# Expert weights in 2 MB slots, and an earlier load of one vector of rows, in a two-block transformer kernel

## The reference, cut to what matters

```
for l in range(DEPTH):                                   # DEPTH = 1
    mod = cond @ w_ada[l] + b_ada[l]                     # 6 x 1024 columns
    sh_m, sc_m, g_m, sh_f, sc_f, g_f = jnp.split(mod[:, None, :], 6, axis=-1)
    h = _rms(x, norm_mix[l]) * (1.0 + sc_m) + sh_m
    proj = h @ w_in[l]
    ...
    x = x + g_m * (mixed @ w_out[l])
    h = _rms(x, norm_ffn[l]) * (1.0 + sc_f) + sh_f
    x = x + g_f * _moe(h, w_router[l], b_router[l], w_gu[l], b_gu[l], w_dn[l], b_dn[l])
```

## Time and profile before

| what | value |
|---|---|
| median of 3 runs | 2108.74 us (2106.86 to 2115.24) |
| the profiled execution | 2115.58 us |
| its span | 2113.9 us |
| PE busy | 1990.8 us (94%) |
| DVE, ACT busy | 597.1 us, 409.4 us |
| DMA | 582.22 MB, 275 GB/s over the span |
| granted PE clock, mean | 0.972 |

### The profile page before, as it was taken

How to read it: one execution, slowest core, us unless ns; L and a number is a source line. 1 busy time by engine, 2 the same in 40 slices (tenths; PEclk the granted TensorE clock), 3 DMA queues, 4 the chain that set the end, 5 groups by cost and what they waited for, 6 DMA issues and landing times.

```text
span 2113.9 us, 23652 instructions
## 1 busy us (share of the span) xinstructions
PE 1990.8 (94%) x9060; PEld 1130.5 (53%) x9060; DVE 597.1 (28%) x1240; ACT 409.4 (19%) x868; POOL 93.0 (4%) x166
## 2 busy tenths in 40 slices
PE   6889999999899998899899988999999999999998
PEld 2665877433333333333233333756888456668863
DVE  1277522222211221112112211443333025433311
ACT  2124321211010111111011111243221023421110
POOL 0000000000000000000000000110000011000000
PEclk9989999999999999999999999999999999999999
DMA  9564557899999999999999998252544333344430
GB/s 376 154 224 166 170 191 288 349 420 420 421 421 420 421 420 421 421 421 420 421 421 421 421 421 352 100 199 87 178 145 158 139 130 134 122 143 159 148 141 31
DMA packets 160453, 582.22 MB, mean 275 GB/s; under 512 B 12936, under 2 KB 59144, under 8 KB 110080
## 3 DMA queue, kind: packets, MB, share of 16 engines
q1 hardware_dynamic: 155312, 574.71, 69.2%
q0 software_dynamic: 5072, 6.56, 1.4%
HBM read 578.60 MB, written 2.62 MB: 275 GB/s over the span
## 4 chain that ended last, share of the span: by engine, by line
PE 72%; DMA 21%; SPq 5%; ACT 1%; issue 1%; DVE 1%; POOL 0%; DVEq 0%; ACTq 0%
PE psum L358 52%; DMA work<-w_gu 9%; DMA ring<-w_gu 9%; PE psum L607 9%; PE psum L654 8%; SPq L466 5%; DMA gain_rows<-b_ada 2%; PE psum L2077 1%; PE psum L644 1%; DMA ring<-w_in 1%; PE psum L633 1%; DMA ring<-w_ada 0%; ACT work L2398 0%; PE psum L1027 0%; PE psum L560 0%
## 5 line engine op out<-in xcount | busy, mean ns | idle before, releaser
L358 PE MATMUL psum<-normed,ring 128*128 128x256 f32 (+1 forms) x2432 | 510.4, 372 | 0.2 <-PE psum L358 0.2
L358 PEld LDWEIGHTS psum<-normed,ring 128*128 128x128 f32 x2432 | 445.1, 192 | 61.7 <-issue 5.0
L607 PE MATMUL psum<-work,normed 128*64 128x512 f32 x1024 | 241.2, 629 | 38.6 <-DMA work<-w_gu 38.6
L607 PE MATMUL psum<-ring,normed 128*64 128x512 f32 x1024 | 237.5, 620 | 32.3 <-DMA ring<-w_gu 31.7
L358 PE MATMUL psum<-ring,work 128*128 128x512 f32 (+1 forms) x592 | 249.8, 581 | 0.1
L358 PE MATMUL psum<-work 128*128 128x128 f32 (+7 forms) x1152 | 186.1, 334 | 18.6 <-DVE gain_rows L1567 14.6
L607 PEld LDWEIGHTS psum<-work,normed 128*64 128x64 f32 x1024 | 77.0, 145 | 200.7 <-issue 200.7
L358 PEld LDWEIGHTS psum<-ring,work 128*128 128x128 f32 x592 | 111.7, 190 | 130.6 <-issue 129.3
L358 PEld LDWEIGHTS psum<-work 128*128 128x128 f32 (+2 forms) x1152 | 135.7, 187 | 80.7 <-issue 52.9
L607 PEld LDWEIGHTS psum<-ring,normed 128*64 128x64 f32 x1024 | 76.4, 143 | 190.7 <-issue 189.0
L358 PE MATMUL psum<-ring,normed 128*128 128x512 f32 (+2 forms) x400 | 160.5, 556 | 2.2 <-DMA ring<-w_in 1.7
(11 more groups left out here) (303 smaller groups left out, 1332.4 us busy)
## 6 DMA issues: line engine op xcount, KB each, us to landing
ring<-w_gu SPq DMA_DIRECT2D x128, 1024.0 KB, 26.3
work<-w_gu SPq DMA_DIRECT2D x128, 1024.0 KB, 26.3
ring<-w_dn SPq DMA_DIRECT2D x64, 1024.0 KB, 26.8
work<-w_dn SPq DMA_DIRECT2D x64, 1024.0 KB, 26.8
ring<-w_in SPq DMA_DIRECT2D x25, 2048.0 KB, 12.5
ring<-w_up SPq DMA_DIRECT2D x44, 1024.0 KB, 7.2
ring<-w_ada SPq DMA_DIRECT2D x11, 2048.0 KB, 9.2
ring<-w_down SPq DMA_DIRECT2D x10, 2048.0 KB, 7.7
```

Of the source, the lines that this page charges most:

```text
L358: return pe.matmul(out, lhsT, rhs, start=first, stop=last, **kw)
L607: ins = pe.matmul(b[r], self.hgT[:, o, r], ws[e][:, n0:n0 + 512], start=o == 0, stop=o == EIGHTHS - 1, skip_group_check=True)
```

## The change

1. **Slots of 2 MB.** The weights of a pair come in 12 pieces of 2 MB: quarter q of w_gu of expert e, and half of w_dn. A partition's part is one run of 16 KB. PE still makes the same products in the same order, but waits once for a quarter, and signals its use once (`quarter_used`, `down_half`); a slot is refilled when the slot 8 places before has been used.
2. **First refill and last w_dn half in two pieces.** The first refill (first half of w_dn of the first pair, into the slots of quarter 0) is issued as 2 x 2 pieces of 1 MB: the first two when eighth 0 has been used (`first_eighth`), the other two when the quarter has been. The last w_dn half of the last pair is also issued in pieces of 1 MB, and PE waits for the second pieces apart (`rest_in`).
3. **b_ada rows.** `bias_rows(2)` is the first DMA of POOL's queue and waits only for `("win", 0)`, the first slice of w_in.
4. **Bias line.** The line goes to DRAM once (8 x 384 numbers) and is spread there by a DMA from DRAM to DRAM, 128 rows of 3072 numbers; `toeplitz` reads from that.
5. **Turns.** The turn of the probabilities stands before `ada(6)` and `ada(7)`; `attend(1)` stands behind the first two turns of x; `y_transposes(1)` stands before the last `attn_out`. The bank list and ACT's list are put in the same order.

```diff
-EIGHTHS, DOWN_PARTS = 8, 4
+QUARTERS = 4
 def pair_slots(u):
-    return [("gu", u, o, e) for o in range(EIGHTHS) for e in range(2)] + [("wd", u, m, e) for m in range(DOWN_PARTS) for e in range(2)]
+    return [("gu", u, q, e) for q in range(QUARTERS) for e in range(2)] + [("wd", u, half, e) for half in range(2) for e in range(2)]
...
+        if kind == "gu":
+            src = io["w_gu"][bass.ds(2 * p + e, 1), part * 256:part * 256 + 256, :]
+            sp.dma_start(slot(S.no(name), 2, 2048), src.rearrange("a (p k) n -> p (a k) n", p=P)).then_inc(*S.fills(*name))
+            return
...
+    def load_by_halves(self, sp, io, S, slot, names, p, between=None):
+        for m in range(2):
+            for name in names:
+                part, e = name[2:]
+                src = io["w_dn"][bass.ds(2 * p + e, 1), part * 512:part * 512 + 512, :].rearrange("a (p m k) n -> m p (a k) n", p=P, m=2)
+                sp.dma_start(slot(S.no(name), 4, 1024)[:, 2 * m:2 * m + 2], src[m])\
+                    .then_inc(*(S.fills(*name) if m == 0 else (self.rest_in[part], 16)))
+            if m == 0 and between is not None:
+                sp.wait_ge(*between)
...
+            if i < MOE_SLOTS + 2 and skip:
+                if name[3] == 0:
+                    sp.wait_ge(self.first_eighth, 1)
+                    self.load_by_halves(sp, io, S, slot, PAIR_SLOTS[i:i + 2], pair, (self.quarter_used, 1))
+                continue
             if name[3] == 0:
-                earlier = i - PIECES
+                earlier = i - MOE_SLOTS
...
+        for q in range(QUARTERS):
+            pe.wait_ge(self.rows_ready, it * 4 * TWINS + (4 * u + q + 1))
+            ws = []
+            for e in range(2):
+                pe.wait_ge(*S.ready("gu", u, q, e, it=it))
+                ws.append(mem.slot(S.no(("gu", u, q, e)), 2, 2048))
+            if q < QUARTERS - 1:
+                for k in range(2):
+                    for c in range(4):
...
+        pool.wait_ge(*S.ready("win", 0))
+        bias_rows(2)
         pool.wait_ge(line_ready, 1)
-        pool.dma_start(line, line_sb.unsqueeze(1).to_broadcast([HEADS, P, 384])).then_inc(line_out, 16)
-        bias_rows(2)
+        pool.dma_start(line_one.rearrange("a (h n) -> (a h) n", h=HEADS), line_sb).then_inc(line_out, 16)
         pool.wait_ge(line_out, 16)
+        pool.dma_start(line, line_one.to_broadcast([P, HEADS * 384])).then_inc(line_out, 16)
+        pool.wait_ge(line_out, 32)
         pool.wait_ge(*B.ready("kT", 1))
...
         logits(0)
         by_token(("z", 0), wait_slot("win", 6), 0, 512)
+        turn_probs(0)
         ada(6)
         attend(0)
...
         by_token(("z", 1), wait_slot("win", 7), 0, 512)
+        turn_probs(1)
         ada(7)
-        attend(1)
         for t in range(NT):
+            if t == 1:
+                attend(1)
...
         attn_out((2,))
         ada(11)
+        y_transposes(1)
         attn_out((3,))
         mod_rows(11)
-        y_transposes(1)
```

More of the change, by code:

```diff
@@ L455, in __init__, with load @@
         assert A.at <= WORK - (MOE_SLOTS - SLOTS) * SLOT
-    def load(self, sp, io, S, name, p):
+    def load(self, sp, io, S, slot, name, p):
         kind, u, part, e = name
[L460 to L466, removed]
@@ L471, in last_use, with load_weights @@
+    def load_weights(self, sp, io, S, B, slot, pair, it, skip=0, last=False):
         def last_use(name, it, turn):
             kind, u, part, e = name
[L474 to L477, removed]
+            if kind == "gu" and part < QUARTERS - 1:
+                return self.quarter_used, (it - turn) * 3 * TWINS + (3 * u + part + 1)
+            if kind == "wd" and part == 0:
+                return self.down_half, (it - turn) * TWINS + (u + 1)
@@ L595, in weights_and_biases, with column @@
                           start=False, stop=False, skip_group_check=True)
[L597 to L602, removed]
+        def column(c, q, k, ws):
             b = psum[:, B.no(columns[c])]
@@ L645, in products @@
                       start=True, stop=False, skip_group_check=True)
[L646 to L651, removed]
+        for half in range(2):
+            pe.wait_ge(*B.released("aT", u, half, it=it))
+            ws = []
+            for e in range(2):
+                pe.wait_ge(*S.ready("wd", u, half, e, it=it))
+                ws.append(mem.slot(S.no(("wd", u, half, e)), 4, 1024))
+            for k, dh in [(k, dh) for k in range(4) for dh in range(2)][0:8 - 4 * half] + [(k, dh) for dh in range(2) for k in (2, 3)][0:4 * half]:
+                if (k, dh) == (2, 0):
+                    pe.wait_ge(self.rest_in[half], it * 32 * TWINS + 32 * (u + 1))
                 for e in range(2):
                     r = slice(e * CAP, (e + 1) * CAP)
[L654 to L656 removed]
+                    ins = pe.matmul(psum[r, B.no(("dn", u, dh))], self.actT[:, 4 * half + k, r], ws[e][:, k, dh * 512:dh * 512 + 512],
+                                    start=False, stop=half == 1 and k == 3, skip_group_check=True)
+                if half == 1 and k == 3:
                     ins.then_inc(*B.fills("dn", u, dh))
[L658 to L659 removed]
+            if half == 0:
+                ins.then_inc(self.down_half, 1)
     def act_part(self, act, B, psum, it, u):
@@ L1903, in second_block @@
     bank_free = [sem(f"bank_free_2_{b}") for b in range(BANKS)]
+    slot_full = [sem(f"slot_full_2_{b}") for b in range(SLOTS)]
     LL = range(LAYERS)
```

139 lines of the change are left out of this document (72 added, 67 removed).

## The result

The changed kernel takes **2078.47 us** (median of four executions, 2075.91 to 2079.24), the kernel before 2110.76 us on the same chip (four executions). The ratio is 0.9848, with a 95% interval of 0.9826 to 0.9870. 2077 us and a gain of 31.9 us were forecast; the gain is 32.3 us.

The account below looks back on a forecast made before the run. DMA engines were taken to bound the experts, PE mostly the rest. 18.3 + 3.6 + 12 - 2 = 31.9 us off the 2108.7 us median gave 2077 us, range 2066 to 2096 us.

Parts of the forecast that it names:

- The rows and the line: Front: loading the b_ada rows early removes PE's wait before the last `dots` group and its after-effects, 18.3 us; spread line 0 us.
- The 14.64 us: Front: PE's standstill before the fourth `dots` group, while DVE waits for the b_ada rows, goes whole.
- the 0.85 us: Front: the last `dots` group's four matmuls follow the twelve before in 0.3 us, not 1.15 us.
- The 2.8 us of slow clock: Front: the 64 matmuls after the wait take 13.98 us at full clock, not 16.79 us.
- late next: Front: next candidate is the w_in slice issued at 89.38 us, wanted at about 119 us, expected in at 109 us.
- The bounds of the margins: Front: w_in slice in at 109 us, spread line by 97 us, early load covered, DVE not the new wait.
- The turns: First block: three PE waits for ACT's copies, before `O` 0, `O` 1 and `ys`, go: 3.6 us, at least 0.
- The rate: Experts: 16 KB rows move 1.5% faster than 8 KB rows; 13.4 us worked out, 12 us taken, bounds 0 and 14.
- The dip: Experts' first refills: the next refill waits for the whole quarter and the DMA queue runs empty, 2 us lost, between 0 and 3.
- The rival of little gain in rate: Experts: 16 KB rows bring only 0 to 0.6%, total 2084 to 2089 us; chance 0.18.
- the slower one: Experts: long rows move worse, so the rate falls; chance 0.10, of which 0.06 slower overall.
- The front's wait: Front: the wait returns as late w_in, late `bias` or DVE's pace; half the 18.3 us left gives 2086 us; chance 0.10.

Follow-up runs that it names:

- a_slots_only: Kernel before with only the 2 MB slots and split loads, front as before: 2094.56 us, ratio 0.9932.
- a_turns_only: Kernel before with only the turns of the first block in their new order: 2106.97 us, ratio 0.9993.
- c_old_turns: Changed kernel with the turns of the first block back in their old order: 2077.97 us, ratio 0.9857.
- a_line_only: Kernel before with only the bias line written to DRAM once and spread there, b_ada rows still behind its first write: 2091.06 us, ratio 0.9917.
- a_rows_only: Kernel before with only the b_ada rows loaded first, bias line written as before: 2099.37 us, ratio 0.9949.
- c_after_again: Changed kernel measured again without an edit, in the third group: 2076.06 us, ratio 0.9845.
- b_8k_rows: Changed kernel with each 2 MB expert load as two rows of 8 KB per partition, not one of 16 KB: 2088.75 us, ratio 0.9906.
- b_plain_first: Changed kernel with the first refill of the experts not split: 2076.80 us, ratio 0.9846.
- c_second_split_again: Changed kernel with the second refill of the experts split as well, measured a second time: 2074.60 us, ratio 0.9839.

## Why the prediction was right, point by point

**The rows and the line (18.3 us).** Right in size, a little large. From the first `dots` product to the second group of 64 matmuls it takes 20.40 us, before 38.86: 18.5 us. The 14.64 us and the 0.85 us are gone whole. The 2.8 us of slow clock are the part that moves: a_slots_only and a_turns_only, whose front keeps the wait, take 15.74 and 15.93 us for the 64 matmuls that took 16.79, so there it is 1.8 to 2.0 us. c_old_turns differs from a_slots_only in the rows and the line alone, and has its 64 matmuls behind the scan's sums 102.80 us after the first `dots` product and not 120.00: 17.2 us. Where the prediction was incomplete is the cause. It says that the load's move takes the wait away, and takes the line as a thing that must not be late. Over the same stretch a_line_only, too, takes 102.80 us, so the line alone gives all of it (16.5 us in the times); the move alone gives 13.0 of the 17.2 us (8.2 in the times), and the move on top of the line nothing. The old line costs through what stands beside it, the rows and the slices of w_in alike. What the prediction said would be late next came true in a_rows_only only: 2.23 us for `ring<-w_in` at 122.53 us.

**The bounds of the margins** held: the slice of w_in is in at 89.19 + 12.7 = 101.9 us (109 were allowed), the spread line at 80.72 + 8.0 = 88.7 us (97), the bias is read right behind `kT` 1 at 119.89 us. The early load costs nothing that shows: the second product of the front starts without a wait. DVE did not become the pace, but it is near it: the chain's share of DVE is 3% where it was 1%, and PE's new wait of 0.31 us is for DVE.

**The turns (3.6 us).** The term measured 3.5 us where the clock stays up, and 1.9 us by c_after_again: a half-clock stretch that costs 1.7 us stands behind the moved turns in eight of nine traces of the new order, and in one of five of the old one (the kernel before itself). The prediction had no term for it. Why it comes so much oftener in the new order was not settled; PE is busy 4.00 of 4.00 us in it, and ahead of it come some 14 us of small turns and sums (matmul groups of 0.4 to 2 us, with waits of 0.2 to 0.9 us) in both orders.

**The rate (12 us).** Right, a little small. The changed kernel and b_8k_rows differ in the row length alone. From the first product to the last quarter of w_gu the one takes 901.07 us (c_after_again), the other 914.46 (351.96 to 1266.42 us): 13.4 us, which is what the prediction had worked out before it took 12. The row of b_8k_rows:

```profile
1266.42 7.09 PE L620 MATMUL psum<-work,normed 128*64 128x512 f32 x32 [1.16 <-DMA work<-w_gu]
```

Rows of 2, 4, 8 and 16 KB moved at 386, 409, 421 and 427 GB/s. A sixteenth of each is 84.9, 160.2, 311.3 and 613.9 ns for a row, or 37.73 ns per 1024 bytes and 9.3 to 10.2 ns fixed; the line drawn through 2 and 8 KB held at the other two. The Trainium skill (*DMA: Bandwidth & Descriptors*, section on why small descriptors are slow) gives about 3 cycles fixed beside one for 32 bytes; the forecast by it was 5 us. The section also names 32 bytes of metadata that go with each descriptor, which that forecast left out; as one more cycle they make it 7 us, an estimate by that page. The runs disagree with both: they show a gain of 13.4 us.

**The dip (-2 us).** Seen as forecast: 370 to 374 us has 229 GB/s, which is (1 - 229/427) x 4 = 1.9 us without loads. Up to the last quarter b_8k_rows, with the coarse slots and rows of 8 KB, takes 1.8 us more than the kernel before (912.68), which is this term measured by itself (1.1 to 2.1 us against the four traces of the old slots). What was expected later of the split first refill, in b_plain_first, was too much: it buys 1.5 us (902.60 us up to the last quarter without it, 901.07 with it) of the 3.4, since the second refill then sets the end.

**Not in the sum: 1.2 to 2.7 us at the end of the stage.** From the last quarter's first product to the second block it is 33.09 us before, 31.87 in the changed kernel and 30.41 in c_after_again. The rows of PE tell why. Behind one wait of 5.31 us the 32 matmuls of that quarter take 9.77 us, and 9.0 to 9.8 us in all four traces of the old slots. In the changed kernel's first profile they take 8.55 us behind a wait of 2.69 us. In c_after_again they take 7.09 us behind 1.20 us, and in c_second_split_again 7.09 us behind 2.70, both at full clock:

```profile
1242.87 8.59 PE L620 MATMUL psum<-ring,normed 128*64 128x512 f32 x32 [2.69 <-DMA ring<-w_gu]
1252.66 7.09 PE L620 MATMUL psum<-work,normed 128*64 128x512 f32 x32 [1.20 <-DMA work<-w_gu]
```
```profile
1248.57 7.09 PE L621 MATMUL psum<-work,normed 128*64 128x512 f32 x32 [2.70 <-DMA work<-w_gu]
```

In the other pairs the slow clock hides behind the loads; in the last one nothing hides it. With the coarser slots PE's idle time is in three parts, and the last quarter is at full clock in eight of ten such traces. Behind the same wait of 2.7 us it comes at either clock, so the 1.5 us between 31.87 and 30.41 do not follow from the wait; why the clock differs stays open.

**The sum and the rivals.** Of the forecast's 31.9 us the front has 21.9 and the experts 10.0. The profiles differ by 23.55 and 12.78. 1.3 us of the front are slow clock at the gather before the experts, which the trace of before had and that of after has not; the rest is the 22.25 us up to `ys`, 18.65 up to the second group of 64 matmuls and 3.60 behind it. The rival of little gain in rate is refuted by b_8k_rows, the slower one by the 427 GB/s. The front's wait did not come back; 4 us of it (2.23 and 1.8 us) did in a_rows_only, without the spread line. That the median's gain (32.3) is less than that of the profiles (36.5) comes from the profile of before, which is a long one of its kind: a_slots_only, with the same front, has the first product of the experts at 370.73 us, 6.7 us earlier. Against that front c_after_again gains 19.1 us (351.59 us; 17.2 + 1.9 by the terms above) and not 21.9, and its experts take 14.3 us less than the 945.77 (13.4 - 1.8 + 2.7) and not 10.0. So the front was forecast some 3 us too high and the experts some 4 us too low, and that the sum comes within 0.4 us of the measured gain is in part luck.

## What to carry to other kernels

A slow DMA can cost more than its own landing time: look at what lands slowly beside and behind it, and try to give it another shape before you move the others out of its way. In a stage that is bound by loads, a fixed cost for each row worked out from two rates of one trace foretold the third and the fourth here. The refills right after the start have to come evenly: splitting the first alone moved more than half of the dip to the next. The version with both refills split has the shortest expert stage here (929.16 and 929.43 us) and the lowest times (2073.34 and 2074.60 us), though the intervals of the latter overlap with the changed kernel's.

## What was unexpected of the hardware

PE's granted clock falls to half for a few us in stretches in which PE is busy all the time. In the kernel before (same columns as above):

```profile
220.00:224.00 4.00, 4.00 (x14) 3.26 (x14) 3.42 (x11) 0.00 (x0) 0.00 (x0) 0.57 1.04 398
260.00:268.00 8.00, 8.00 (x55) 7.87 (x54) 3.92 (x6) 0.60 (x1) 2.09 (x3) 0.80 0.86 269
```

a_slots_only has the clock at 1.00 in both places. From the 64 matmuls behind the scan's sums to `ys` it takes 301.84 - 219.68 = 82.16 us, the kernel before 307.40 - 220.24 = 87.16 us: 5.0 us, from the clock alone. Part of the spread of the executions (8.4 us in the kernel before) can well come from this; that was only argued. A difference of 3 us between two single profiles of such a front says little until the clock of each stretch has been looked at.

A pair takes 1% longer than the mean rate gives (24 MB at 427 GB/s are 58.9 us, measured 59.5), and so with 8 KB rows before (59.8 and 60.4) and 4 KB rows (61.5 and 62.15). What makes up this 1% stays open.
